# Making the high part of each weight tile on GpSimd in four casts of two chunks instead of one cast of eight

## What is computed

```python
def run_group(x, ...):
    h = x
    for layer in range(2):
        xn = rmsnorm(h, gain)
        if layer == 0:      # gated DeltaNet (4 heads) and retention (4 heads) behind one projection
            mix = mixer_ab(xn, ...)
        else:               # mLSTM matrix memory (4 heads)
            mix = mixer_c(xn, ...)
        h = h + mix
        xn = rmsnorm(h, gain)
        hid = relu(xn @ w_up)            # 1024 -> 4096
        h = h + (hid * hid) @ w_down     # 4096 -> 1024
    return rmsnorm(h, final_gain)
```

## Time and profile before

| | us |
|---|---|
| median of 3 runs | 2911.99 |
| the 3 runs | 2911.37 to 2913.46 |
| the profiled execution | 2915.2 |
| its span | 2913.4 |
| granted clock of TensorE, mean | 0.98 of 2.4 GHz |

### The profile page before, as it was taken

One profiled execution on the slowest core, in us unless ns is written; L12 is line 12 of the kernel. 1 busy time (PEld: TensorE's weight loads), 2 busy tenths in 40 slices (PEclk: granted clock), 3 DMA queues, 4 the chain that ended last, 5 costly groups with the idle time before them and its releaser, 6 DMA issues.

```text
span 2913.4 us, 43523 instructions
## 1 busy us (share of the span) xinstructions
PE 2790.0 (96%) x17734; PEld 2690.8 (92%) x17734; DVE 1442.8 (50%) x2623; ACT 349.1 (12%) x588; POOL 923.9 (32%) x1227
## 2 busy tenths in 40 slices
PE   8889898999999999999999999998999999999997
PEld 7878787799899999999999999997899999999997
DVE  5756758554676235152356335436576153261443
ACT  3211302112240000000001011112230000000001
POOL 3220302222234333343333422223234343333341
PEclk9999999999999999999999999998999999999998
DMA  3110101111221111111112122122211111111111
GB/s 121 51 46 14 52 15 52 60 45 52 69 88 44 51 44 51 44 44 51 44 59 88 57 73 75 39 66 74 98 37 49 46 44 51 44 44 47 48 44 73
DMA packets 46304, 160.12 MB, mean 55 GB/s; under 512 B 7198, under 2 KB 9118, under 8 KB 45102
## 3 DMA queue, kind: packets, MB, share of 16 engines
q1 hardware_dynamic: 30528, 111.20, 12.1%
q10 hardware_dynamic: 15598, 46.27, 4.4%
HBM read 138.81 MB, written 18.64 MB: 54 GB/s over the span
## 4 chain that ended last, share of the span: by engine, by line
PE 60%; issue 12%; POOL 6%; DVE 3%; ACT 1%; DMA 0%; POOLq 0%; ACTq 0%; DVEq 0%; SPq 0%
PE proj L375 52%; PE bank L452 6%; POOL w_lo L310 4%; POOL w_hi L307 1%; PE proj L430 1%; PE bank L449 1%; DVE x_lo L815 0%; POOL pool_gate L306 0%; PE bank L439 0%; DVE s L925 0%; DVE h L1402 0%; DVE s L773 0%; PE bank L416 0%; DVE s L924 0%; DVE s L923 0%
## 5 line engine op out<-in xcount | busy, mean ns | idle before, releaser
L375 PE MATMUL proj<-x_hi,w_hi 128*128 128x344 f32 x4716 | 1548.6, 328 | 56.7 <-DVE s L773 32.1
L375 PE MATMUL proj<-x_lo,w_hi 128*128 128x344 f32 x4716 | 1517.5, 322 | 0.0
L375 PE MATMUL proj<-x_hi,w_lo 128*128 128x344 f32 x4716 | 1516.8, 322 | 0.0
L375 PEld LDWEIGHTS proj<-x_hi,w_hi 128*128 128x128 f32 x4716 | 896.1, 190 | 82.8 <-issue 64.7
L375 PEld LDWEIGHTS proj<-x_lo,w_hi 128*128 128x128 f32 x4716 | 896.8, 190 | 1.7 <-issue 0.2
L375 PEld LDWEIGHTS proj<-x_hi,w_lo 128*128 128x128 f32 x4716 | 896.0, 190 | 0.0
L310 POOL TENSOR_TENSOR w_lo<-w_raw,w_hi 128x256 fp32r<-128x256 f32 x808 | 665.6, 854 | 16.2
L306 POOL TENSOR_TENSOR pool_gate<-pool_gate 1x1 f32<-1x1 f32 x204 | 54.2, 266 | 1933.7 <-PE proj L375 1885.6
L1249 DVE TENSOR_TENSOR h<-h,proj 128x344 f32<-128x344 f32 x144 | 74.0, 514 | 453.1 <-PE proj L375 453.1
L1239 DVE TENSOR_TENSOR mlp_t<-proj,rbc 128x344 f32<-128x344 f32 x192 | 99.2, 517 | 274.8 <-PE proj L375 258.2
L307 POOL CAST w_hi<-w_raw 128x1024 fp32r<-128x1024 f32 x202 | 208.0, 1030 | 0.0
(11 more groups left out here) (270 smaller groups left out, 1880.4 us busy)
## 6 DMA issues: line engine op xcount, KB each, us to landing
w_raw<-w_all SPq DMA_DIRECT2D x204, 512.0 KB, 3.5
h<-x SPq DMA_DIRECT2D x8, 516.0 KB, 9.3
s<-rows_a ACTq DMA_DIRECT2D x8, 516.0 KB, 4.7
h<-x ACTq DMA_DIRECT2D x8, 516.0 KB, 6.8
h_spill<-h ACTq DMA_DIRECT2D x8, 516.0 KB, 2.6
h<-h_spill ACTq DMA_DIRECT2D x8, 516.0 KB, 7.3
y<-h ACTq DMA_DIRECT2D x8, 516.0 KB
sample_C<-state_c ACTq DMA_DIRECT2D x4, 1024.0 KB, 6.8
```

The source lines that it names most:

```text
L375: last = nc.tensor.matmul(PJ[:, tt, 0:TT], w[slot][:, k, :], x[:, k, tt * TT:(tt + 1) * TT], start=(at == 0 and j == 0), stop=(at == len(o ...
```

## The change

The cast to w_hi is put into a loop like that of the low part: four instructions of two chunks (256 columns) each in a tile of 8 chunks, two in the tail tile of 4. The last of them raises `w_hi_done`, for which GpSimd waits as before, and then come the four pieces of the low part as before. The constant `LO_PIECE` becomes `PIECE`, with the same value.

```diff
-LO_PIECE = 2
+PIECE = 2
...
                 nc.gpsimd.tensor_tensor(gate[0:1, 1:2], gate[0:1, 0:1], gate[0:1, 0:1], ALU.mult)
-                nc.gpsimd.tensor_copy(hi[:], src).then_inc(w_hi_done, 1)
+                for k in range(0, chunks, PIECE):
+                    last = nc.gpsimd.tensor_copy(hi[:, k:k + PIECE, :], src[:, k:k + PIECE, :])
+                last.then_inc(w_hi_done, 1)
                 pool.wait_ge(w_hi_done, 2 * i + t + 1)
-                for k in range(0, chunks, LO_PIECE):
-                    last = nc.gpsimd.tensor_tensor(lo[:, k:k + LO_PIECE, :], src[:, k:k + LO_PIECE, :],
-                                                   hi[:, k:k + LO_PIECE, :].bitcast(F32), ALU.subtract)
+                for k in range(0, chunks, PIECE):
+                    last = nc.gpsimd.tensor_tensor(lo[:, k:k + PIECE, :], src[:, k:k + PIECE, :],
+                                                   hi[:, k:k + PIECE, :].bitcast(F32), ALU.subtract)
                 last.then_inc(w_split, 1)
```

## The result

The changed kernel takes 2921.76 us in the median of 6 runs, before 2912.72 in 6 beside it: 1.0034 times as long, 95% interval 1.0024 to 1.0045. It is slower by 0.3 to 0.4%, 9 to 13 us. The forecast was 2907.0 and the range 2902 to 2914. What happened is rival D, which had a chance of 0.04: VectorE doesn't get its turn between the casts.

A forecast was written before the change was run, and what follows sets the result against it. TensorE, busy 96% of the span, was taken as the bound, with gaps in the mixers; 3.0 + 0.7 + 1.3 + 0.7 + 0 - 0.4 - 0.3 = 5.0 us of gain gave 2907.0 us, range 2902 to 2914.

The forecast's parts named there:

- rival D: GpSimd keeps its turn through four casts; VectorE waits 1.41 us, not 1.03, at some 8 places; 2914 to 2915; chance 0.04.
- the one on VectorE's turn: On the shared port, VectorE and GpSimd take turns, one instruction each, so VectorE gets in after 0.34 us, not 1.03.
- The price of a turn: What one cast piece costs a VectorE operation: 0.12 us, or 0.25 at the first piece's start; bounds 0 and 0.39.
- L907 to L911: Three operations in three DeltaNet heads: the 0.99 us gap closes in each, 3.0 us of gain.
- L925: Before the drain at 573.4: cast's cost falls from 0.85 to 0.12 in a 3.69 us gap, 0.7 us of gain.
- L1223: Last mLSTM head: four operations end 1.6 us sooner in a 1.64 us gap; 1.3 us of gain (0.5 to 1.64).
- L1119: At 1695.7: the cast's 0.78 becomes 0.12 ahead of a 2.79 us gap; 0.7 us of gain (0.4 to 0.9).
- L891 before the drain: Eight short operations in three heads, before a drain TensorE waits for: 0 us (-1 to +1).
- L815: At 750.9: low pieces come 0.38 us later and hit one more of the chain; a loss of 0.4 us.
- Tile 0: Kernel start, where TensorE has nothing to do yet and the longer split isn't hidden: 0.3 us of loss (0 to 0.4).
- The cover for GpSimd's longer split: GpSimd's extra 0.38 us in each of 203 tiles is hidden by idle time before the gates, except in tile 0.
- the clock: After long gaps TensorE runs at 1.2 GHz; changed gaps may drop or add such stretches: 2 us either way.

The follow-up runs named there:

- e16: High part as an addition of zeros that waits for GpSimd's own gate, then three casts, against one cast before: 2902.10 us against 2912.54, ratio 0.9967.
- e18: e16's kernel without the wait: addition and three casts back to back; 2937.22 us against 2913.78 of before, ratio 1.0076.
- e4: High part made by four additions of a column of zeros, against the one cast of before: 2946.88 us, ratio 1.0126.
- e8: High part made by four additions of 128 zeros a row, read whole as second input, against the one cast of before: 2969.91 us in a single run.
- e17: The changed kernel itself, unaltered, run again against before: 2925.73 us, ratio 1.0043.
- e1: The changed kernel with a wait and a one-element multiplication between the cast pieces: 2915.71 us against 2911.75 of before, ratio 1.0016.
- e15: The changed kernel with a wait on a second one-element gate instruction ahead of its four casts: 2918.84 us against 2912.54 of before, ratio 1.0021.

## Why the prediction was wrong

The step that failed is the one on VectorE's turn. From L909's and L911's 1.65 us beside low pieces I took it that the two engines take turns, one instruction each, and priced a cast piece at 0.12 us. The runs showed that a run of casts without a wait gives up no turn (0 of 99), so that L909 took 2.47 us, not 1.35. What I held against rival D, that low pieces overlap in the same way and VectorE does get in between them, was true and didn't carry over. The low pieces differ from the casts in two ways: they are subtractions, and the first of them waits for GpSimd's own cast, where the first cast piece follows the gate without a wait. The earlier trace rows has that wait: the first low piece starts 1.11 us after the cast, which lasts 1.03. e16 and e18 show that a waiting addition is enough to make casts behind it yield, e4 and e8 that without a wait the kind counts too. The price of a turn was right where VectorE gets one: behind a cast, e16's L916 takes 1.31 us, 0.08 more than alone. D's price was right as well, 0.38 us an encounter; its sum was for idle time alone.

The Trainium skill ("SBUF — State Buffer", section "Who interferes with whom") says that the holder of the shared port pair keeps it for the whole instruction and the other blocks fully. I had weighed it as too hard on the change. In the change VectorE blocks even longer than that, through four instructions (L909 takes 2.47 us, alone 1.23); in e16 it blocks for one at a time (1.53 and 1.31).

Point by point, each against the profiled execution:

1. L907 to L911: forecast +3.0 us of gain. The waits went from 3.0 to 5.5 us: each grew from 0.99 to 1.4, and the same gap opened in a fourth head as well.
2. L925: forecast 0.7 of gain, 3.69 to 3.0 us. It became 4.46, a loss of 0.77, two encounters of 0.38 (L1100 and L927).

```profile
582.16 2.46 DVE L927 TENSOR_TENSOR s<-s,s 128x1032 f32<-128x1032 f32 x1
...
585.32 0.62 PE L377 MATMUL proj<-x_hi,w_hi 128*128 128x344 f32 x1 [4.46 <-DVE s L775]
```

3. L1223: forecast 1.3 of gain. The casts now miss L1225 and hit L853 behind it, whose pair takes 2.82 us instead of 1.46; the gap went from 1.64 to 3.44.

```profile
2103.96 2.82 DVE L853 TENSOR_TENSOR x_lo<-mix,x_hi 128x344 fp32r<-128x344 f32 x2
...
2106.88 0.63 PE L377 MATMUL proj<-x_hi,w_hi 128*128 128x344 f32 x1 [3.44 <-issue]
```

4. L1119: forecast 0.7 of gain. The gap fell by 2.0 us, from 2.79 to 0.81, for another reason: the tile's split starts later against VectorE's work, and the casts miss L1121 (0.70 us) and meet L1124 alone (2.47).
5. L891 before the drain: forecast 0, with 1 us either way for the three heads. The three gaps grew from 6.87 to 7.66, 7.63 and 7.64, together 2.3 us: outside the bound.
6. L815: forecast 0.4 of loss. The gap went from 2.63 to 3.03 us: right. Tile 0: forecast 0.3 of loss (up to 0.4). The first matmul came at 10.57 instead of 9.86 us, but 0.3 of that is a load that landed later: from the gate behind the load it is 4.54 us before, and 4.94 in both profiled executions of this kernel (the other is e17's), a loss of 0.4.

The cover for GpSimd's longer split held: after tile 0 TensorE waits for no split that it didn't wait for before.

The other mis-sized term is the clock, at 2 us either way. It was 7.7, nearly twice the idle time that was lost. Part of it follows a longer gap directly. Over 13 us around the drain wait, which takes 6.87 us in before and 7.66 in the change, the rows of before and then of the change are

```profile
213.00:226.00 13.00, 6.75 (x34) 6.78 (x35) 12.77 (x23) 4.14 (x5) 3.98 (x6) 0.74 0.16 49
...
216.00:229.00 13.00, 6.20 (x23) 6.23 (x24) 12.77 (x23) 4.29 (x5) 4.53 (x9) 0.61 0.17 53
```

That is some 6.8 us at 1.2 GHz before and 10.2 in the change. It is so in all three heads, in e17's execution too. Three times 3.4 us at half the clock are 5.1 of the 7.1 us by which the clock's share grew from one profiled execution to the other (58.1 to 65.1 by their clock records). Part of it comes behind gaps whose length didn't change. The wait ahead of L452 in that head is 2.08 us in both kernels; here are its row and the clock around it, of before and then of the change:

```profile
253.86 1.51 PE L452 MATMUL bank<-s,s 128*128 128x128 f32 x9 [2.08 <-DVE s L984]
...
250.00:262.00 12.00, 9.75 (x79) 8.94 (x78) 8.15 (x20) 0.00 (x0) 0.00 (x0) 1.00 0.00 0
```

```profile
257.77 1.51 PE L454 MATMUL bank<-s,s 128*128 128x128 f32 x9 [2.08 <-DVE s L986]
...
254.00:266.00 12.00, 9.75 (x65) 8.94 (x64) 7.37 (x19) 0.00 (x0) 0.00 (x0) 0.86 0.00 0
```

The same gap, the same 9.75 us busy in 12 (with x65 matmuls for x79, since some run at the lower level), and 1.00 against 0.86. So the clock's share doesn't go by the sum of the idle time: e1, with less of it, lost 9.4 us to the clock, and e15, with no more, 6.1; e16 has lost none. What puts a stretch at 1.2 GHz behind one such gap and not behind another isn't settled by these runs.

What also stays open is the mechanism of the wait. That an addition of full size which waits makes the casts behind it yield is shown (e16 against e18), that a one-element instruction which waits doesn't, too (e15). Why isn't, nor why additions and subtractions without a wait yield in most places and casts in next to none.

## What to carry over

Cutting a GpSimd instruction in pieces helps VectorE only if the pieces yield; look in the trace for one piece that is stretched, and don't take it from other pieces on the same engine. Here a run of casts that starts without a wait held VectorE to its end, and one whose first piece was of full size and waited for a semaphore of GpSimd's own gave the turn up after each: an addition and three casts with that wait are 0.33% faster than before, without it 0.76% slower. Where TensorE's clock moves with its gaps, give idle time and the clock's share apart, over many runs, before a gain of a few us is promised.

## What the runs showed of the hardware

- Four casts issued back to back, 0.39 us each, start 0.345 us apart and hold VectorE for 1.42 us; eight of 0.28 us hold it for 1.94. None of 99 and none of 102 VectorE operations got in between; in runs of additions without a wait 173 of 185 and 234 of 253 did (e4, e8).
- A cast takes 0.284 us for 128 columns, 0.392 for 256, 0.606 for 512 and 1.029 for 1024: 0.18 us and 0.83 ns a column, as worked out from two sizes.
- An addition of a repeated column takes 0.60 us for 256 columns, with a second input that is read 0.73: the subtraction's 0.74.
